# Two hybrid blocks on one core: 512-wide products in the late column tiles, sums added at eviction, and small steps in three chains

## What is computed

```python
h = rmsnorm(x, norm_g) * (1 + scale) + shift
proj = h @ w_in                                     # 1024 x 10240
q, k, v, g_attn, cb, cc, cx, g_conv, m_attn, m_conv = jnp.split(proj, IN_OFFSETS, axis=-1)
y_attn = (moba_attention(q, k, v) * silu(g_attn)) @ w_o_attn
y_conv = (cb * causal_conv3(cc * cx) * silu(g_conv)) @ w_o_conv
merged = sigmoid(m_attn) * y_attn + sigmoid(m_conv) * y_conv
out = rmsnorm(x + gate * (merged @ w_out), final_g)
```

## Time and profile before

| | us |
|---|---|
| median of 3 runs | 1026.37 (1025.7 to 1026.7) |
| profiled execution, its own time | 1025.78 |
| span of its instructions | 1024.0 |
| PE busy | 984.7 (96%) |
| DVE busy | 391.9 (38%) |
| ACT busy | 376.8 (37%) |
| POOL busy | 121.6 (12%) |
| DMA, mean over the span | 301 GB/s |

### The profile page before, as it was taken

The page is one execution under the profiler, slowest core; times in us unless marked ns, Lnnn a source line. Parts: engine busy times, 40 slices in busy tenths (PEclk is TensorE's granted clock), DMA queues, the critical chain, the costliest instruction groups (busy, mean ns, idle before and its releaser), DMA issues. The chain is left out here.

```text
span 1024.0 us, 16905 instructions
## 1 busy us (share of the span) xinstructions
PE 984.7 (96%) x7389; PEld 764.7 (75%) x7389; DVE 391.9 (38%) x750; ACT 376.8 (37%) x612; POOL 121.6 (12%) x81
## 2 busy tenths in 40 slices
PE   7999999999999999979999999999999999999997
PEld 6887789976555555545555555558989999999995
DVE  4456356853222211121222111127334444774475
ACT  4546656551111111111111111226445555554443
POOL 1110121020000000000000000002321111341122
PEclk9999999999999999989999999999999999999998
DMA  9974395889999999999999999998445544445401
GB/s 303 359 264 170 108 346 205 310 313 375 424 425 426 425 422 426 426 420 425 425 425 424 425 425 424 424 400 307 178 164 188 189 172 165 164 165 191 159 1 42
DMA packets 74859, 308.08 MB, mean 301 GB/s; under 512 B 5600, under 2 KB 12176, under 8 KB 58392
## 3 DMA queue, kind: packets, MB, share of 16 engines
q1 hardware_dynamic: 70848, 302.10, 74.5%
q10 hardware_dynamic: 3928, 4.80, 1.4%
HBM read 305.82 MB, written 2.63 MB: 301 GB/s over the span
## 5 line engine op out<-in xcount | busy, mean ns | idle before, releaser
L788 PE MATMUL bank<-hTR,wR 128*128 128x256 f32 x2520 | 315.4, 286 | 5.6 <-DVE wR L1305 3.1
L788 PEld LDWEIGHTS bank<-hTR,wR 128*128 128x128 f32 x2520 | 306.7, 192 | 9.6 <-issue 5.5
L788 PE MATMUL bank<-ring,arena 128*64 128x256 f32 (+3 forms) x1680 | 229.4, 439 | 6.8 <-issue 6.8
L1305 DVE TENSOR_TENSOR wR<-ring,wR 128x1024 fp32r<-128x1024 f32 x126 | 158.9, 1267 | 131.3 <-ACT wR L1886 130.9
L1886 ACT ACTIVATE wR<-ring 128x1024 fp32r<-128x1024 f32 x161 | 168.3, 1054 | 110.5 <-PE bank L788 108.7
L788 PEld LDWEIGHTS bank<-ring,arena 128*64 128x64 f32 (+2 forms) x1680 | 115.3, 137 | 102.7 <-issue 59.3
L788 PE MATMUL bank<-arena 128*64 128x256 f32 (+7 forms) x1178 | 166.2, 406 | 0.8 <-DVE small L1437 0.7
L1311 DVE SCALAR_TENSOR_TENSOR arena<-bank,small,arena 128x256 f32<-128x256 f32 x32 | 15.5, 484 | 346.5 <-ACT arena L2064 346.5
L2035 ACT ACTIVATE arena<-bank,small 64x512 f32<-64x512 f32 x62 | 42.4, 684 | 280.0 <-PE bank L788 279.6
L788 PEld LDWEIGHTS bank<-arena 128*64 128x64 f32 (+3 forms) x1178 | 92.1, 144 | 62.2 <-issue 28.1
L2270 POOL TENSOR_TENSOR wR<-ring,wR 128x1024 fp32r<-128x1024 f32 x35 | 85.5, 2441 | 320.1 <-ACT wR L1886 320.1
(11 more groups left out here) (209 smaller groups left out, 816.0 us busy)
## 6 DMA issues: line engine op xcount, KB each, us to landing
ring<-in_w SPq DMA_DIRECT2D x39, 2048.0 KB, 21.5
ring<-in_w_in SPq DMA_DIRECT2D x29, 2048.0 KB, 8.1
arena<-in_w SPq DMA_DIRECT2D x25, 2048.0 KB, 19.5
ring<-in_w SPq DMA_DIRECT2D x42, 1024.0 KB, 19.7
arena<-in_w SPq DMA_DIRECT2D x22, 1024.0 KB, 20.8
ring<-in_w_ada SPq DMA_DIRECT2D x6, 2048.0 KB, 7.9
ring<-in_w_o SPq DMA_DIRECT2D x2, 2048.0 KB, 12.1
ring<-in_w_o_attn SPq DMA_DIRECT2D x2, 2048.0 KB, 7.8
```

The costliest lines, as they stand in the source:

```text
L788: return pe.e.matmul(o, l, r, start=start, stop=stop)
L1305: return eng.tensor_tensor(o, a, b, op)
```

## The change

- **Wide tiles.** In the 48 late tiles (p8, p9, p14 to p19, oa, oc), high weights times high *and* low activations is one product of 512 columns into a bank of its own: high x high in its first half, high x low in its second. Low x high is added to the first half as before. So 2 matmuls a step instead of 3, with the same number of columns; six banks in turn, one a tile, instead of three for two tiles each.
- **Sums at eviction.** A new step "sum" follows every wide tile: ACT copies the bank's second half to SBUF, DVE adds the first half to it. The two sums of a pair are then passed through silu or sigmoid by ACT from SBUF to SBUF (p14 to p19). "mix" multiplies in SBUF.
- **Start.** The first piece is split before turn1. DVE scales its half of x before it copies the constants. POOL does one power beforehand.
- **End of the experts.** The second half of the last result is scaled by DVE.
- **Tail.** ACT's scaling of the first 128 rows is cut in two, the second part behind the squares of the other rows.

```diff
@@ first O1 steps @@
+        O1.more()
         for j2 in range(4):
             PB.use(("hT1", j2), 2 + j2)
             O1.add("turn1", j2)
-            if j2 == 0:
-                O1.more()
@@ late column tiles and output projections in O2 @@
+        n_PR = PR.n % 3
+        PR = Turn([0, 1, 6, 2, 3, 4])
+        PR.n = n_PR
         for nm in ("p8", "p9", "p14", "p15", "p16", "p17", "p18", "p19"):
             for c2 in range(2):
-                u = PB.use((nm, c2), PR.next())
-                for st in O2.pair(nm, c2, u, "h3"):
+                uses = [PB.use((nm, c2, half), PR.next()) for half in range(2)]
+                for half, st in enumerate(O2.wide_pair(nm, c2, uses, "h3")):
                     O2.add(*st)
+                    O2.add("sum", nm, c2, half)
                 O2.add("evict", nm, c2)
                 for st in side.pop(0) if side else ():
                     O2.add(*st)
         O2.add("final_g")
-        n_PR = PR.n % 3
-        PR = Turn([0, 1, 6, 2, 3, 4])
-        PR.n = n_PR
         for jj in range(4):
             for nm in ("oa", "oc"):
-                u = PB.use((nm, jj), PR.next())
-                for st in O2.pair(f"{nm}{jj // 2}", jj, u, nm):
+                uses = [PB.use((nm, jj, half), PR.next()) for half in range(2)]
+                for half, st in enumerate(O2.wide_pair(f"{nm}{jj // 2}", jj, uses, nm)):
                     O2.add(*st)
+                    O2.add("sum", nm, jj, half)
@@ tensor program @@
+        def wide_tile_pe(pe, i, u, src):
+            h, l = parts(i)
+            x = {"h3": hTR, "oa": aR, "oc": cR}[src]
+            bank = banks[u.bank]
+            may_write(pe, u)
+            pe.wait_ge(*low[i])
+            for j in range(8):
+                if j % 2 == 0:
+                    ready(pe, src, j)
+                if j == 7:
+                    mm(pe, bank[:, 0:256], l[:, j, :], x[:, 0, j, :], False, False)
+                last = mm(pe, bank[:, :].rearrange("p (m t) -> p m t", m=2), h[:, j, :], x[:, :, j, :], j == 0, j == 7)
+                if j < 7:
+                    mm(pe, bank[:, 0:256], l[:, j, :], x[:, 0, j, :], False, False)
+            last.then_inc(piece_done[i][0], 1)
+        def sum_of(nm, c2, half):
+            if nm in ("oa", "oc"):
+                return TM2[c2 % 2][nm == "oc"][:, 256 * half:256 * half + 256]
+            i = int(nm[1:])
+            return {4: cbT, 7: gC, 8: mA, 9: mC}[i // 2][:, 4 * (i % 2) + 2 * c2 + half, :]
@@ vector program: last expert @@
-                return lambda: low(NE // 2 - 1)
+                def finish():
+                    e, q = NE - 1, NE // 2 - 1
+                    u = P.of["y", r, e]
+                    filled(v, u)
+                    v.wait_ge(S["scat"], 16 * g + q - 1)
+                    ts(Yb[q % 2][64:128, 512:1024], banks[u.bank][64:128, :], RW[64:128, e // EB % 2, e % EB, 0:1], None,
+                       ALU.mult).then_inc(u.free, 1)
+                    low(q)
+                return finish
@@ vector program: second_steps @@
+                elif what == "sum":
+                    u, dst = U_[a], sum_of(*a)
+                    v.wait_ge(s_part, sum_no[a])
+                    tt(dst, banks[u.bank][:, 0:256], dst, ALU.add).then_inc(u.free, 1)
...
                 elif what == "mix":
                     jj = a[0]
-                    T, ua, uc = TM2[jj % 2], U_["oa", jj], U_["oc", jj]
-                    filled(v, U_["p19", 1])
-                    filled(v, ua)
-                    emptied(v, U_["p16" if jj < 2 else "p17", jj % 2])
-                    tt(T[0], banks[ua.bank][:, :], flat2(mA, 2 * jj), ALU.mult).then_inc(ua.free, 1)
-                    filled(v, uc)
-                    emptied(v, U_["p18" if jj < 2 else "p19", jj % 2])
-                    tt(T[1], banks[uc.bank][:, :], flat2(mC, 2 * jj), ALU.mult).then_inc(uc.free, 1)
+                    T = TM2[jj % 2]
+                    for m, (nm, gates_) in enumerate((("oa", mA), ("oc", mC))):
+                        for half in range(2):
+                            emptied(v, U_[nm, jj, half])
+                        v.wait_ge(s_made, 4 + 4 * m + jj + 1)
+                        v.step(tt(T[m], T[m], flat2(gates_, 2 * jj), ALU.mult))
@@ vector program: start @@
+            v.wait_ge(s_rs[1], 1)
+            ts(XS1[:, 1, :], XN[:, 1, :], ss[:, 5:6], None, ALU.mult).then_inc(s_norm[1], 1)
             filled(v, U_["rows"])
             eng.tensor_copy(col[:, :], banks[7][:, 0:NROW]).then_inc(U_["rows"].free, 1)
-            v.wait_ge(s_rs[1], 1)
-            ts(XS1[:, 1, :], XN[:, 1, :], ss[:, 5:6], None, ALU.mult).then_inc(s_norm[1], 1)
@@ scalar program: second_steps @@
-                    elif i in (8, 9):
-                        u = U_[nm, c2]
-                        filled(s, u)
-                        for h in (6, 7):
-                            emptied(s, U_["o2", h])
-                        eng.activation(flat2(cbT, 4 * (i - 8) + 2 * c2), banks[u.bank][:, :], ACT.Copy).then_inc(u.free, 1)
                     elif i >= 14:
-                        u = U_[nm, c2]
-                        filled(s, u)
...
                         dst, f = ((gC, ACT.Silu), (mA, ACT.Sigmoid), (mC, ACT.Sigmoid))[(i - 14) // 2]
-                        eng.activation(flat2(dst, 4 * (i % 2) + 2 * c2), banks[u.bank][:, :], f).then_inc(u.free, 1)
+                        for half in range(2):
+                            emptied(s, U_[nm, c2, half])
+                        x = flat2(dst, 4 * (i % 2) + 2 * c2)
+                        eng.activation(x, x, f).then_inc(s_made, 1)
+                elif what == "sum":
+                    nm, c2, half = a
+                    u, i = U_[a], int(nm[1:]) if nm[0] == "p" else -1
+                    if nm == "oa":
+                        filled(s, U_["p19", 1, 1])
+                    if i < 0:
+                        if c2 > 1:
+                            s.wait_ge(s_m, c2 - 1)
+                    elif i in (14, 15):
+                        emptied(s, U_["p13", 1])
+                    elif i in (16, 17):
+                        s.wait_ge(s_cb, 8)
+                    else:
+                        for h in (6, 7):
+                            emptied(s, U_["o2", h])
+                    filled(s, u)
+                    eng.activation(sum_of(*a), banks[u.bank][:, 256:512], ACT.Copy).then_inc(s_part, 1)
                 elif what == "last_squares":
                     n = a[0]
                     squares(1, n)
-                    if n == 0:
-                        s.wait_ge(s_rs[0], 4)
-                        s.wait_ge(s_fo[0], 1)
-                        eng.activation(XO[:, 0, :], XO[:, 0, :], ACT.Copy, scale=st3[:, 6:7]).then_inc(s_out[0], 2)
+                    s.wait_ge(s_rs[0], 4)
+                    s.wait_ge(s_fo[0], 1)
+                    cs = slice(512 * n, 512 * n + 512)
+                    eng.activation(XO[:, 0, cs], XO[:, 0, cs], ACT.Copy, scale=st3[:, 6:7]).then_inc(s_out[0], 1)
@@ pool program @@
             p.step(eng.memset(mhalf[:, :], -0.5))
+            p.step(eng.memset(small[:, 250:251], 1.0))
             p.settle()
+            p.step(eng.tensor_tensor(small[:, 251:252], small[:, 250:251], mhalf[:, 0:1], ALU.pow))
             rms()
```

More of the change, by code:

```diff
@@ L372, in bass_two_hybrid_blocks @@
                                                            "var", "w1_"))
+        s_made, s_part = sem("made"), sem("part")
         s_gx, s_x2done, s_sq3, s_fo = ([sem(f"{m}{n}") for n in range(NT)] for m in (
@@ L443, in pair, with wide_pair @@
                     yield ("tile", i, use, half, src)
+            def wide_pair(self, nm, c2, uses, src):
+                for half in range(2):
+                    i = self.take(nm)
+                    done_by(i, uses[half])
+                    yield ("wide_tile", i, uses[half], src)
             def chunk(self, nm, uses, src):
@@ L938, in tile_pe @@
             last.then_inc(piece_done[i][0], 1)
+        def wide_tile_pe(pe, i, u, src):
[13 more added lines that the diff above has]
+            last.then_inc(piece_done[i][0], 1)
+        sum_no = {st[1:]: n + 1 for n, st in enumerate(st for st in O2.steps if st[0] == "sum")}
+        def sum_of(nm, c2, half):
[3 more added lines that the diff above has]
+            return {4: cbT, 7: gC, 8: mA, 9: mC}[i // 2][:, 4 * (i % 2) + 2 * c2 + half, :]
         def rows_pe(pe, i, uses, p, src):
@@ L1270, in second_steps_pe @@
                 tile_pe(pe, *a)
+            elif what == "wide_tile":
+                wide_tile_pe(pe, *a)
             elif what == "rows":
@@ L1789, in second_steps @@
                     j = a[0]
-                    emptied(v, U_["p14" if j < 4 else "p15", j % 4 // 2])
+                    v.wait_ge(s_made, j // 2 + 1)
                     v.wait_ge(s_cb, j + 2)
@@ L1796, in second_steps @@
                     jj = a[0]
[L1797 to L1806 removed]
+                    T = TM2[jj % 2]
[4 more added lines that the diff above has]
```

(10 more changed lines are left out.)

11 lines of the change are left out of this document (1 added, 10 removed).

## The result

| | before | changed |
|---|---|---|
| median of 20 runs, us | 1026.75 (1025.69 to 1029.87) | 1029.43 (1026.72 to 1031.25) |
| profiled execution, span | 1024.0 | 1029.5 |
| DVE, ACT busy | 391.9, 376.8 | 407.8, 388.2 |

A forecast was written before the change was run, and what follows sets the result against it. PE's work and the stretches in which PE waits were taken to set the end. Late stage +1.85, start -1.8 and tail -0.15 sum to -0.1 us against 1025.78 profiled, given as 1026.3 for the median; range 1020.5 to 1030.0.

The forecast's parts named there:

- PE work of 48 wide tiles: Late stage: 384 steps at 0.347 us each instead of 0.360, saving 5.1 us of PE work.
- convolution: Four pairs with the convolution: DVE, with the adds, needs 26.4 us against PE's 22.2, so PE waits; +3.3 us.
- s_cb: At p16: the wait for POOL's multiplication moves to the first tile's copy, with a split behind it; +1.1 us.
- mix 0 to 2: Chain from tile's end through sum and mix to the next split takes 6.0 us against PE's 5.55; +1.35 us.
- mix 3: Same chain against two pieces of the last product, 0.55, plus 0.7 from mix 2's lateness; +1.2 us.
- late stage: Sum of PE's saving and the four added waits, from p8 to oc: +1.85 us.
- start: Kernel start: earlier first product, and the clock may stay at 1.00 behind it; -1.8 us.
- end of experts, tail: Half the last scaling moved to DVE: 0; squares of the second rows no longer behind the whole scaling: -0.15 us.
- rival C: Late stage: the wide product, reading two separate pieces, saves no time over two of 256; 1029.6 us, chance 0.10.
- Rival A: Late stage: the adds fit into time when POOL holds DVE anyway, so waits stay small; 1020.7 us, chance 0.22.
- Rival B: Convolution and mixes: POOL's splits hold the sums and what follows; 1031.6 us, chance 0.13.
- PE begins at 12.7: Start: PE's first product begins at 12.7 instead of 13.80 through the earlier split; -1.1 us.

The follow-up runs named there:

- start_alone: The kernel before with only the three start edits (first split ahead of turn1, DVE's scaling ahead of its copy, POOL's power ahead of time): 1025.41 us, ratio 0.9995.
- grouped: The changed kernel with a tile's eight 256-wide products in a row ahead of the last wide one: 1028.22 us, ratio to before 1.0012.
- one_piece: The changed kernel, its 512-wide product reading two neighbouring blocks of the high part as one piece (other numbers): 1029.57 us, ratio to before 1.0027.
- mix_first: The changed kernel with mix 0 to 2 ahead of the sum of oa's second tile instead of behind it: 1027.14 us, ratio to before 1.0006.
- late_alone: The changed kernel without the start's edits: 1030.13 us, ratio to before 1.0042.
- spread: The changed kernel with one convolve step behind each of eight pairs, not two behind four, and the two gate buffers exchanged: 1024.03 us, ratio to before 0.9969.
- narrow_best: The kernel before with the start's edits, the spread convolution and exchanged gate buffers, without wide tiles: 1024.05 us, ratio 0.9972.
- first_split: The kernel before with one start edit only, the first split ahead of turn1: 1025.34 us, ratio 0.9995.
- ahead: mix_first with the split of the last product's third piece also ahead of mix 3: 1026.68 us, ratio to before 0.9999.
- best: The changed kernel with spread, ahead (mix_first in it) and grouped: 1022.45 us, ratio to before 0.9950.
- before_spread: The kernel before with the spread convolution and exchanged gate buffers, no wide tiles: 1024.78 us, ratio 0.9981.

## Why the prediction was wrong

It said no change, 1026.3, with 0.45; the kernel is slower, though within the range. Term by term, against the profiled execution:

| term | forecast | measured |
|---|---|---|
| PE work of 48 wide tiles | -5.1 | -2.9 |
| convolution | +3.3 | +1.8 |
| s_cb | +1.1 | +1.7 |
| mix 0 to 2 | +1.35 | +1.4 |
| mix 3 | +1.2 | +1.1 |
| late stage | +1.85 | +3.14 |
| start | -1.8 | -1.0; -2.1 in start_alone |
| end of experts, tail | 0, -0.15 | 0, 0 |
| a fall of the clock at 230 | not in it | +3.4 (by the two groups of times, in about half of the runs) |

**The step that failed first** is "a step takes 0.227 + 0.120 = 0.347 us". The two durations were read where each kind follows itself; in alternation the two together take 0.3525 us. grouped shows that most of this excess belongs to the alternation, one_piece that none belongs to the two pieces, which rival C had suspected. With the start's gain too high by 0.8, this turned a sum of -0.1 into a loss: the late stage alone came out 1.3 above its forecast, even though its waits together were smaller than forecast (6.0 against 6.95). It was a saving of 13 ns a step, so 6 ns took 2.2 of 5.1 us. Rival C's 13 ns lost were too many and its reason wrong, but its direction was right. The 0.03 to 0.04 us a pair that grouped left above the sum of rows stay unexplained.

**The places of the waits** were right, all four, with DVE or POOL as releaser as named. The convolution's was oversized: "DVE needs 23.03 + 8 x 0.425" took the 23.03 as fixed, though it contained operations held by POOL, and how many are held changes with the order. Before, three were, by 4.7 us in all (2.50 for 0.35 at 883.11, 0.83 for 0.35 at 895.15, a row of two at 896.02 with 3.04 for 1.00); in the changed kernel two, by 2.8 (1.02 for 0.34 at 886.53, 2.47 for 0.35 at 898.14). Rival A's argument was worth half of the term. A part of what was saved there came back at p16: the chain behind the multiplication took 3.95 us (911.15 to 915.10), as forecast (3.8), but the multiplication itself came late, released by DVE: together 3.5 against 4.4 forecast. For mix 3 the size was right by luck: "another 0.7 for mix 2's lateness" was wrong, since in mix_first, without that lateness, the wait stays 1.0, so that the chain, put at 0.55, makes all of it.

Rival B's mechanism, adds held by POOL, is not there: 14 of the 48 adds of the changed kernel begin while a POOL operation runs, and take 0.42 to 0.43 us like the others.

**The start.** The step "PE begins at 12.7" held in start_alone (12.84) and not in the changed kernel's record (13.87). That record is the latest of the eleven with the edit (median 13.09); the three without it have 13.81, 13.89 and 14.47. So the step is right on the whole, by 0.8 where 1.1 was forecast, and this execution missed it. The other part of the term was right in size: from PE's first product to the tenth split it is 22.06 us in before, with the fall, and 20.97 in the changed kernel, without. The identity matrix, for which PE's first products wait, landed at 5.64 instead of 5.21, and PE ran slow for longer. Before, then the changed kernel:

```profile
5.21 3.83 PE L788 MATMUL bank<-ident 128*128 128x128 f32 x18 [5.21 <-DMA ident<-in_k_ident]
...
8.98 0.84 PE L788 MATMUL bank<-ident 128*128 128x128 f32 x6
```

```profile
5.64 4.21 PE L797 MATMUL bank<-ident 128*128 128x128 f32 x18 [5.64 <-DMA ident<-in_k_ident]
...
9.83 1.51 PE L797 MATMUL bank<-ident 128*128 128x128 f32 x6
```

The same six products take 0.84 us in one and 1.51 in the other, which the table by stretch doesn't show (it gives a granted clock of 1.00 for 5 to 14 us in both). The Trainium skill, "TensorE: Matmul & The Clock Gate", section "Part 1: The HAM clock gate (the "warmup" mystery)", says that the number of slow products at a kernel's start changes from run to run. The traces agree: a product took 0.21 us up to 8.5 us before and up to 11.4 in the changed kernel, and 0.11 from then on.

**The clock later on** was left out. The prediction counted the fall at 15 us as a loss that can be taken away. The runs show that in executions without it a fall can come at later pauses, at 72 or 230, once or twice as long, and that nothing behind hides it: from the 55th to the 61st split it is 502.1 us in before, without a fall at 230, 504.0 in one_piece, with a single one, and 505.4 in the changed kernel, with one of twice the length. (One more, between 453 and 460, is in every trace; in late_alone it is a third shorter, and the stretch takes 502.0 there too.)

That the start's edits take away the fall at 15 is not shown. Only before's trace has it. Of the eleven traces with the edit, two have no fall before 400 us (spread, narrow_best), two one near 73 (start_alone, first_split), two at 73 and 230 (ahead, best), and five at 230. Of the other two without the edit, late_alone has none, and before_spread has them at 74 and 231. So the "nearer to the second, because the pause that preceded the fall shrinks by half" of the prediction came true in the trace, but the same happened in late_alone, where PE's wait ahead of its first product was 2.16 us as in before. Shown is where falls came and what they cost. Why one pause is followed by a fall in one execution and not in the next stays open, as does whether the changed kernel has more of them than before.

**DVE beside POOL.** The prediction weighed a rule of the Trainium skill, "GPSIMD Engine Reference", section "1. Specifications", by which a DVE instruction with two SBUF inputs contends with POOL. In the changed kernel that decided little at the mixes: their three operations cover 2.0 to 2.2 us, 0.7 each, as in the earlier trace rows, because POOL's splits met at most the first of them, which then took 0.8. Where a split does fall on a mix, in mix_first, the trace agrees with the rule: 4.09 us instead of 2.01, so 2.1 of the "up to 2.4" that were forecast as lateness, and there it cost PE nothing.

## What to carry to other kernels

Where a saving is a few per cent of an instruction, read its duration in the mix in which it will stand: 13 ns a step shrank to 7.5, mostly by alternation. An operation put between a product and the next preparation of weights costs by the length of the chain at that place, even where the engine has room on average; count the chain for each place, and first move what fills the tight stretch (spread brought 4.7 us with wide tiles and 1.2 without). Do not book a clock's fall as a gain from one trace: look at several traces of both kernels for where it comes, and compare kernels by a stretch without one.

## What was not expected of the hardware

- Matmuls of 512 and 256 columns in turn take 352.5 ns a step, in groups 349, and by their own rows 347.
- Falls of the clock that cost 1.5 to 2 or 3.4 us come at other places in other executions of like kernels, and are as large as the change itself; the late stretch, without one, repeats within 0.01 us between kernels that are alike there.
- A power on POOL issued ahead of time, at 0.94 us, takes 0.55 us, the next one, at 6.94, takes 1.52, and the one behind it 0.55 again. Without the early one it is 1.41 and 0.55. So the long one is not simply the first, and an early one doesn't shorten it; the cause is open.
- A POOL split that meets a DVE operation on SBUF holds it (2.8 us instead of 0.7 in mix_first), while adds that read a bank pass beside it in 0.42 us.
